# A retention and attention step on one core: where the samples' operands, four evictions and five transposes of the retention stand

## The reference, cut to what matters

```python
scores = jnp.einsum('nihd,njhd->nhij', q, k) * decay[None]
intra = jnp.einsum('nhij,njhv->nihv', scores, v)
cross = jnp.einsum('nihd,nhdv->nihv', q, s0) * inner[None, :, :, None]
s1 = s0 * jnp.exp(c * log_gamma)[None, :, None, None] + jnp.einsum(
    'njhd,njhv->nhdv', k * tail[None, :, :, None], v)
# later: (ro - mu) * rsqrt(var + eps), times silu(rg)
```

## Time and profile before

| what | value |
|---|---|
| three runs | 1779.35, 1779.56, 1781.95 us (median 1779.56) |
| profiled execution | 1779.11 us, its span 1777.3 us |
| mean granted TensorE clock | 0.995 of 2.4 GHz |
| PE busy | 1745.1 us, 98% of the span |
| DVE, ACT, POOL busy | 836.1, 517.8 and 946.2 us |
| chain that ended last | PE 90%, DVE 5%, DMA 2% |
| retention tasks, head 0 to last | about 300 to 594 us of the span |

### The profile page before, as it was taken

The page is one execution under the profiler, slowest core; times in us unless marked ns, Lnnn a source line. Parts: engine busy times, 40 slices in busy tenths (PEclk is TensorE's granted clock), DMA queues, the critical chain, the costliest instruction groups (busy, mean ns, idle before and its releaser), DMA issues.

```text
span 1777.3 us, 29822 instructions
## 1 busy us (share of the span) xinstructions
PE 1745.1 (98%) x12458; PEld 1706.3 (96%) x12458; DVE 836.1 (47%) x925; ACT 517.8 (29%) x942; POOL 946.2 (53%) x520
## 2 busy tenths in 40 slices
PE   7999999999999999999999999999999999999998
PEld 7999999898998999999989999999999999999998
DVE  4633322445545144445847787444454444632213
ACT  6533321011110034646102225333333333201003
POOL 3697873323232422232437449988888886344550
PEclk9999999999999999999999999999999999999999
DMA  6342334023132424364734441223222222723122
GB/s 245 107 132 96 109 107 155 27 83 104 46 104 78 159 70 146 123 202 135 213 114 119 132 145 57 72 84 97 79 73 92 71 71 81 279 77 123 57 61 96
DMA packets 164974, 196.51 MB, mean 111 GB/s; under 512 B 7289, under 2 KB 139633, under 8 KB 164889
## 3 DMA queue, kind: packets, MB, share of 16 engines
q1 hardware_dynamic: 137024, 152.72, 26.6%
q10 hardware_dynamic: 27865, 42.56, 7.0%
HBM read 137.27 MB, written 57.99 MB: 110 GB/s over the span
## 4 chain that ended last, share of the span: by engine, by line
PE 90%; DVE 5%; DMA 2%; ACT 1%; issue 1%; POOL 1%; DVEq 0%; ACTq 0%; SPq 0%
PE unit_ps L1035 41%; PE pair_ps L1096 35%; PE unit_ps L1482 4%; PE task_banks L1316 2%; PE task_banks L1289 1%; PE task_banks L1302 1%; PE task_banks L1213 1%; PE task_banks L1190 1%; DVE s_kparts L2299 1%; DMA temp<-x_spill 1%; DVE s_lo L2156 1%; PE task_banks L1197 1%; DVE temp L2640 0%; DVE a_lo L2156 0%; PE task_banks L1185 0%
## 5 line engine op out<-in xcount | busy, mean ns | idle before, releaser
L1035 PE MATMUL unit_ps<-a_hi,w_part 128*128 128x344 f32 x2592 | 526.3, 328 | 3.9 <-DVE a_lo L2142 3.5
L903 POOL TENSOR_TENSOR w_part<-w_raw,consts 128x1024 fp32r<-128x1024 f32 (+1 forms) x69 | 166.3, 2410 | 607.3 <-PE unit_ps L1035 551.0
L1035 PEld LDWEIGHTS unit_ps<-a_hi,w_part 128*128 128x128 f32 x2592 | 424.4, 189 | 12.9 <-issue 9.9
L1035 PE MATMUL unit_ps<-a_lo,w_part 128*128 128x344 f32 x1296 | 276.2, 322 | 0.0
L1096 PE MATMUL pair_ps<-a_hi,slots_a 128*128 128x258 f32 x1536 | 258.1, 283 | 1.6 <-DVE a_lo L2156 1.3
L1035 PEld LDWEIGHTS unit_ps<-a_lo,w_part 128*128 128x128 f32 x1296 | 219.8, 190 | 0.0
L1096 PEld LDWEIGHTS pair_ps<-a_hi,slots_a 128*128 128x128 f32 x1536 | 216.1, 190 | 2.0 <-DVE a_lo L2156 1.5
L906 POOL TENSOR_TENSOR w_part<-w_raw,w_part 128x1024 fp32r<-128x1024 f32 (+1 forms) x71 | 189.7, 2672 | 15.0 <-DVE a_lo L2142 9.7
L1096 PE MATMUL pair_ps<-a_lo,slots_b 128*128 128x258 f32 x768 | 139.8, 284 | 0.5 <-issue 0.3
L1583 ACT ACTIVATE snap<-pair_ps 128x516 f32<-128x516 f32 x128 | 77.0, 602 | 214.2 <-PE pair_ps L1096 213.8
L2165 DVE TENSOR_TENSOR h_out<-pair_ps,snap 128x516 f32<-128x516 f32 x64 | 44.5, 695 | 198.0 <-ACT snap L1583 128.4
(11 more groups left out here) (284 smaller groups left out, 3012.1 us busy)
## 6 DMA issues: line engine op xcount, KB each, us to landing
w_raw<-in_w_in SPq DMA_DIRECT2D x38, 512.0 KB, 3.9
h_spill<-h_out SPq DMA_DIRECT2D x11, 1032.0 KB, 4.9
raw_a<-in_w_gate_up SPq DMA_DIRECT2D x11, 1024.0 KB, 7.0
raw_b<-in_w_gate_up SPq DMA_DIRECT2D x11, 1024.0 KB, 5.1
gate_spill<-stage ACTq DMA_DIRECT2D x16, 516.0 KB, 2.7
a_lo<-h_spill SPq DMA_DIRECT2D x15, 516.0 KB, 5.3
w_raw<-in_w_down SPq DMA_DIRECT2D x16, 448.0 KB, 3.6
att_in<-att_spill ACTq DMA_DIRECT2D x3, 2048.0 KB, 7.6
```

The lines of the kernel that those rows point to most:

```text
L903: pool.tensor_tensor(part[:, 0], raw, one, ALU.mult).then_inc(w_high, 1)
L1035: mm = pe.matmul(unit_ps[s][:, n, 0:PIECE], w_part[:, slot, w, k0 + by * k, :], x[:, k, n * PIECE:(n + 1) * PIECE], start=(k == 0 and part ...
```

## The change

- DVE makes the samples' operands in `ret_slot(h, 1)`, right behind the state sums and so ahead of the eviction of unit 1, and no longer in `ret_slot(h, 2)` behind that eviction. This holds for all four heads.
- ACT copies the four `OUT_` tasks in slot 1 and no longer in slot 2. In heads 0 to 2 its list stays as it was, since nothing stands between the two slots. In the last head the copies now stand ahead of `spill(1)`.
- The last head's `TURN` tasks run in pairs ahead of k steps 3 and 4 of unit 4, and `TS` ahead of step 5; before, one each ahead of steps 4, 5, 6 and 7, and `TS` ahead of step 1 of unit 5.

```diff
-TURN_LAST = {(4, 4): (TURN,), (4, 5): (TURN + 1,), (4, 6): (TURN + 2,), (4, 7): (TURN + 3,), (5, 1): (TS,)}
+TURN_LAST = {(4, 3): (TURN, TURN + 1), (4, 4): (TURN + 2, TURN + 3), (4, 5): (TS,)}
@@ ACT, ret_slot(h, j)
-                for x in {0: (*range(VT, KT_), KS), 2: range(OUT_, OUTER), 3: (OS,)}.get(j, ()):
+                for x in {0: (*range(VT, KT_), KS), 1: range(OUT_, OUTER), 3: (OS,)}.get(j, ()):
@@ DVE, ret_slot(h, j), at the end of "if j == 1:"
                                 empty(ins, RET_NUMBER[h, x])
                                 emptied(x)
-                if j == 2:
                     emptied(KS)
                     eye = const("eye8").rearrange("p (a b) -> p a b", a=SAMPLES)
                     step(dve.tensor_copy(s_khigh[:], s_ktok[:]))
```

## The result

| | before | after |
|---|---|---|
| median of the runs, us | 1779.45 (4 runs, 1778.03 to 1781.95) | 1765.82 (4 runs, 1764.65 to 1766.57) |
| profiled execution, its span, us | 1779.11, 1777.3 | 1765.72, 1763.9 |
| mean granted TensorE clock | 0.995 | 0.997 |

The ratio is 0.9921, 95% interval [0.9904, 0.9938]: the medians differ by 13.6 us, and the interval allows 11 to 17 us. 1766.0 us had been forecast. The span of the profiled execution fell by 13.4 us, and the sum of the prediction was 13.34 us.

The account below looks back on a forecast made before the run. PE, busy for 98% of the span, was taken as the bound. Removing its four waits was to save 2.47 + 4.02 + 2.49 + 4.36 = 13.34 us from 1779.11 us; forecast 1766.0 us, range 1764.0 to 1770.0.

Parts of the forecast that it names:

- Part 1: Retention, heads 0 to 2: samples' operands made before unit 1's eviction end PE's waits at line 1207, gaining 8.98 us.
- Part 2: Retention, last head: ACT's output copies ahead of the spill end PE's wait at line 1197, gaining 4.36 us.
- Part 3: Last head's transposes: pairing them earlier changes nothing, value 0, bounds -0.2 to +0.2 us.
- The clock: Retention, heads 1 and 3: low clock after PE's gaps counted as 3.2 us of the gain, 1.5 and 1.7.
- Rival A: Sample attention or last rows: a later gap draws the low clock, 1.5 to 3.2 us come back; chance 0.14.
- Rival C: Unit 3, each head: late eviction of unit 1 makes PE wait, about 16 us more, 1795 us; chance 0.04.

Follow-up runs that it names:

- the statistics instruction: Kernel after the change with 17 extra one-input statistics instructions between casts and masks in DVE's operand chain; 1772.88 us, ratio 0.9960.
- the run with the gated products late: Kernel after the change with the two gated products of the head before moved behind the OUTER evictions; 1765.46 us, ratio 0.9923.
- the tripled masks: Kernel after the change with the three mask instructions (s_kparts) done three times over; 1788.35 us, ratio 1.0052.

## Why the prediction was right

**Part 1** holds in mechanism and size. Alone it gave 8.5 us by the medians and 9.1 us by the ratio where 8.98 were worked out, the chain ended within 0.1 us of its forecast, and the reason given for the long casts was shown three ways (held, replaced by ACT's, and in the new place). The eviction of unit 1 was not late at all, where up to 2.2 us were allowed. The casts have one SBUF input each; why they contend and the statistics instruction does not, no run shows.

**Part 2** holds, and so does its condition, that the wait would move to OUTER if part 1 failed: the run with the copies alone shows that move, at 2.24 us where about 2.5 were given.

**Part 3**, valued at 0 with bounds of 0.2 us, took the same 51.57 or 51.58 us of PE with and without the change. The time alone says only that it is within 1.6 us of nothing.

**The clock.** 3.2 of the 13.34 us were counted as clock. Head 1 lost 4.02 us where a low clock followed its gap and head 0 lost 2.47 us where none did. After the change nothing in the retention is under 1.00. Which gaps draw the low clock varies: in all four traces with four gaps of 2.2 to 2.5 us it was two of them, in heads 1 and 3 or in heads 1 and 2. The prediction counted its two from one execution; the others show the same number. Rival A, that a later gap draws the low clock instead, did not come about in the profiled execution. Its mechanism exists, and the argument against it, that the later gaps are 1.3 us and less, was wrong: the gaps at line 1096 reach 1.7 us, come in twos, and drew the low clock in 8 of 12 traces. They did so with the operands in the old place and in the new, and at under 0.1 us in the run with the gated products late, so A's price of 1.5 to 3.2 us did not come with it. That the spans of the two profiled executions differ by just the sum is in part luck: neither drew it there, and in one of the other traces it cost 1.2 us. The Trainium skill, page "TensorE: Matmul & The Clock Gate", section "What's actually happening", says that the gate follows activity on a clock of its own that does not start with the kernel. The two traces of the kernel before agree: their gaps fell in the same places of the program and drew the low clock at different ones.

**What was mis-sized** is the contention of the gated products. The prediction priced it as one or two splits 0.8 us later. POOL's instruction was indeed 0.8 us longer, but DVE paid more: 5.68 instead of 2.37 us a pair. The pair ended at 406.66, 1.2 us before the first OUTER result could be evicted, so it cost nothing; the margin was just large enough. The same omission made the expectation for the tripled masks wrong by 21 us and more.

**Rival C** has a wrong sum, which changed nothing: 348.4 - 326.5 less an eviction of 1.23 us is 20.7 and not 21.8 us. Its 28 us and 7.3 us go by 20.7.

## What to carry to other kernels

Before moving a chain of instructions into an engine's idle stretch, look at who else works in the old and the new stretch: here the same nine instructions took 8.5 us beside POOL's weight split and 5.4 us ahead of it, and an instruction that is too long and ends just behind another engine's (0.07 to 0.3 us here) may be waiting for it though the trace calls it busy. Holding it back until the other is done, as was done with the casts, tells. Two waits on one path are not a sum: undo one at a time and see whether the other takes its place. Measure what a wait costs between two fixed instructions of the waiting engine, not by the length of the wait, which left out 4 of 13 us here.

## What the runs showed of the hardware that was not expected

- DVE instructions with two SBUF inputs and one-input casts stretch beside POOL's elementwise instructions, by up to 2.2 us each; the statistics instruction, with one input, does not (427 to 430 ns, beside the split and ahead of it), and neither do evictions from PSUM with one SBUF input (1.23 us at 332.57 in the kernel after, beside the split that starts at 332.61, and 1.23 us at 340.22 with the statistics instructions, where POOL idles).
- POOL pays less than DVE: 3.24 or 3.25 us instead of 2.37 where it started behind a DVE instruction of two SBUF inputs and 1.2 us or more, which can have 128 rows (the gated products) or 8 (the tripled masks); next to nothing (2.36 to 2.42 us) where it met the casts or subtractions of 0.2 to 0.4 us.
- A low TensorE clock (1.2 GHz for some microseconds) followed 0 of 7 gaps of 1.1 and 1.55 us in these traces, 10 of 19 gaps of 2.2 to 2.5 us, all 3 of 2.9 us and all 4 of 3.4 us, counting only the gaps of 1 us and more ahead of lines 1197 and 1207. Where it did, it cost about 1.5 us more in the kernel before. At line 1096, where two shorter gaps (1.1 to 1.7 and 0.3 or 0.8 us) stand 1 us apart, it followed in 8 of 12 traces, so short gaps that stand close together are not safe either.
